# Two layers of a hybrid backbone on one core: latent products dealt by unit, one modulation block moved into the differential attention, three weight loads in another order

## The reference, cut to what matters

```
for l in range(2):
    mod = split(silu(c) @ ada_w[l] + ada_b[l], 6)        # c and c_ctx: shift, scale, gate, twice
    h = modulate(rmsnorm(x), mod[0], mod[1])             # 512 latent and 256 context tokens
    p = h @ w_in[l]                                      # SSD | differential attention | MLA columns
    d = for 4 heads, for each 128 queries:
        (softmax(q1 k1) - lam * softmax(q2 k2)) @ v      # latents see 768 keys, context sees 256
    cq, ckv, k_rope = latent columns of p                # 352 columns, and 16 of dt for the SSD
    a = softmax(q(cq) k(ckv, k_rope)) @ v(ckv)           # MLA, 4 heads
    s = bidirectional SSD over conv(p)
    x += mod[2] * rmsnorm([s, d, a] @ w_out[l])
    x += mod[5] * rmsnorm(expert_choice_ffn(modulate(rmsnorm(x), mod[3], mod[4])))
```

## Time and profile before

| | us |
|---|---|
| median of 3 runs | 2262.08 |
| lowest, highest | 2249.24, 2265.17 |
| the profiled execution's own time | 2259.05 |
| its span in the profile | 2257.2 |

### The profile page before, as it was taken

One profiled execution on the slowest core, in us unless ns is written; L12 is line 12 of the kernel. 1 busy time (PEld: TensorE's weight loads), 2 busy tenths in 40 slices (PEclk: granted clock), 3 DMA queues, 4 the chain that ended last, 5 costly groups with the idle time before them and its releaser, 6 DMA issues. The chain is left out here.

```text
span 2257.2 us, 25394 instructions
## 1 busy us (share of the span) xinstructions
PE 1962.4 (87%) x10710; PEld 947.2 (42%) x10710; DVE 618.3 (27%) x1149; ACT 522.1 (23%) x1039; POOL 211.1 (9%) x225
## 2 busy tenths in 40 slices
PE   4988999989959999999997999999794977777775
PEld 2655465544423333333334766655342322322222
DVE  2246462253241111111104355522623000000002
ACT  4134452434200000000005145523331000000002
POOL 1400000020011111111101000000100000000000
PEclk9988999989969999999998999999896998998988
DMA  9510401403069999999999113106117999999997
GB/s 345 154 37 1 168 1 41 184 1 110 31 231 380 402 394 394 399 396 394 395 389 321 38 38 135 34 1 224 38 57 297 368 401 401 401 406 401 401 401 261
DMA packets 166371, 534.54 MB, mean 237 GB/s; under 512 B 10600, under 2 KB 19122, under 8 KB 166258
## 3 DMA queue, kind: packets, MB, share of 16 engines
q1 hardware_dynamic: 148112, 487.39, 55.4%
q0 software_dynamic: 16480, 40.21, 6.4%
q10 hardware_dynamic: 1666, 5.31, 0.6%
HBM read 507.72 MB, written 25.17 MB: 236 GB/s over the span
## 5 line engine op out<-in xcount | busy, mean ns | idle before, releaser
L2504 PE MATMUL ps<-ring,arena 128*64 128x512 f32 x1056 | 252.1, 631 | 43.3 <-DMA ring<-in_w_up 29.0
L2504 PE MATMUL ps<-arena 128*64 128x512 f32 x892 | 217.0, 636 | 29.0 <-DMA arena<-in_w_up 29.0
L1914 PE MATMUL ps<-arena,ring 128*128 128x256 f32 (+1 forms) x640 | 208.6, 484 | 8.9 <-ACT arena L848 6.0
L2504 PEld LDWEIGHTS ps<-ring,arena 128*64 128x64 f32 x1056 | 81.3, 145 | 202.8 <-issue 202.8
L1914 PEld LDWEIGHTS ps<-arena,ring 128*128 128x128 f32 x640 | 121.6, 193 | 84.3 <-issue 66.0
L1835 DVE TENSOR_TENSOR arena<-arena,ps 128x512 f32<-128x512 f32 x32 | 22.0, 687 | 453.1 <-ACT arena L1208 453.1
L2433 PE MATMUL ps<-ring,arena 128*128 128x512 f32 x320 | 139.6, 594 | 0.8 <-DVE arena L1721 0.8
L2504 PEld LDWEIGHTS ps<-arena 128*64 128x64 f32 x892 | 70.3, 147 | 165.5 <-issue 165.5
L700 POOL DMA_INDIRECT expert_sums<-arena,small x32 | 52.4, 1639 | 855.7 <-ACT arena L1215 824.2
L2558 PE MATMUL ps<-ring,arena 128*64 128x512 f32 x544 | 122.3, 594 | 0.7 <-ACT arena L1222 0.7
L1208 ACT ACTIVATE arena<-ps 128x512 f32<-128x512 f32 x32 | 19.1, 597 | 439.5 <-PE ps L2504 439.5
(11 more groups left out here) (323 smaller groups left out, 2468.5 us busy)
## 6 DMA issues: line engine op xcount, KB each, us to landing
ring<-in_w_gate SPq DMA_DIRECT2D x35, 2048.0 KB, 21.4
ring<-in_w_down SPq DMA_DIRECT2D x34, 2048.0 KB, 22.5
ring<-in_w_up SPq DMA_DIRECT2D x31, 2048.0 KB, 15.4
arena<-in_w_down SPq DMA_DIRECT2D x25, 2048.0 KB, 23.2
ring<-in_ada_w SPq DMA_DIRECT2D x24, 2048.0 KB, 11.3
arena<-in_w_gate SPq DMA_DIRECT2D x24, 2048.0 KB, 20.6
arena<-in_w_up SPq DMA_DIRECT2D x23, 2048.0 KB, 14.9
ring<-in_w_in SPq DMA_DIRECT2D x6, 2048.0 KB, 13.9
```

What stands on the lines that cost most here:

```text
L1914: ins = mm(o[0:n, c0:c1], w[:, k, col:col + n], hT[:, k, c0:c1], start=k == 0, stop=k == KD - 1)
L2504: ins = mm(ps[0][hf * 64:hf * 64 + 64, col:col + 512], xl[e % 2][:, at:at + CAP_L], w[c][:, hf * 512:hf * 512 + 512], start=b + c == 0, st ...
```

## The change

Four things.

- `latent_products` no longer spreads each tile's eight products evenly. Each head (4 in layer 0, 4 in layer 1) does one tile, and a table deals its products to the head's units. In layer 0, where units 0 and 1 of a head are the context tiles: (0, 4, 3, 1, 0, 0), twice (2, 3, 2, 1, 0, 0), and (2, 2, 1, 1, 1, 1). Before it was (0, 1, 2, 1, 2, 2) and three times (1, 1, 2, 1, 1, 2). In layer 1: (0, 3, 3, 2) instead of (0, 2, 3, 3), the rest is (2, 2, 2, 2) as before.
- The DVE and ACT steps of the first pair of latents start in step 6 instead of step 1.
- Block 0 of part 1 moves from the stage between into the differential attention: its rows between the scores of unit 0 and the latent products of tiles 0 and 1, its columns behind those products. The job table and ACT's order follow; in ACT's order of the stage between, the rows of block 1 now come ahead of the wait for `o_ss`.
- Three loads change places: with block 0's buffer free early, SP issues the last block of part 1 during the differential attention, ahead of the X columns of w_in, and the B columns of w_in ahead of the third block of part 2.

```diff
-                        ("qk", 4), ("rot", 4), ("v", 2), ("datt", 4 * DH * q + 1),
-                        ("pre", 7), ("mq", 3), ("mrot", 2), ("mk", 2), ("mv", 2),
+                        ("qk", 4), ("rot", 4), ("v", 2), ("datt", 4 * DH * q + 2),
+                        ("pre", 6), ("mq", 3), ("mrot", 2), ("mk", 2), ("mv", 2),
...
-    order = [("score", 0, 0), ("score", 0, 1), ("latents", 0, 0), ("score", 1, 0), ("score", 1, 1)]
+    order = [("score", 0, 0), ("score", 0, 1), ("block", 0, 0), ("latents", 0, 0), ("score", 1, 0), ("score", 1, 1)]
...
-    ends = [(n - 1) * f // 4 + 1 for f in range(5)]
-    for f in range(4):
-        if ends[f] <= u < ends[f + 1]:
-            w, s = ends[f + 1] - ends[f], u - ends[f]
-            return 2 + f, 8 * s // w, 8 * (s + 1) // w
-    return None
+    h, i = divmod(u, n // DH)
+    share = {6: ((0, 4, 3, 1, 0, 0), (2, 3, 2, 1, 0, 0), (2, 3, 2, 1, 0, 0), (2, 2, 1, 1, 1, 1)),
+             4: ((0, 3, 3, 2), (2, 2, 2, 2), (2, 2, 2, 2), (2, 2, 2, 2))}[n // DH][h]
+    return (2 + h, sum(share[:i]), sum(share[:i + 1])) if share[i] else None
...
-    return [(1, (n - 1) // 2 + 2)[i] + k for k in range(4)] if i < 2 else [n] * 4
+    return [(6, (n - 1) // 2 + 2)[i] + k for k in range(4)] if i < 2 else [n] * 4
...
-    return (b, 7 + b, (12, 13, 15, 16)[b])[part]
+    return (b, (7, 8, 9, 11)[b], (12, 13, 14, 16)[b])[part]
...
-                for b, src in enumerate(srcs):
+                for b in [*range(10), 11, 10, 12, 13, 15, 14, *range(16, PRE_BLOCKS)]:
+                    src = srcs[b]
...
                 map_exps(0)
+                rows_out(l, 1, 0)
                 j = unit("latents", 0)
...
+                columns_out(l, 1, 0)
                 map_exps(1)
...
                 turned_latents(0)
+                rows_out(l, 1, 1)
+                turned_latents(1)
                 act.wait_ge(*a.next(S["o_ss"]))
                 rsqrt(rstd[:, 4 * q[0]:4 * NT], ssum[:, 4 * q[0]:4 * NT], DV, S["o_rstd"])
-                rows_out(l, 1, 0)
-                turned_latents(1)
-                columns_out(l, 1, 0)
-                rows_out(l, 1, 1)
+                columns_out(l, 1, 1)
+                rows_out(l, 1, 2)
                 turned_latents(2)
-                rows_out(l, 1, 2)
-                columns_out(l, 1, 1)
                 rows_out(l, 1, 3)
...
                 map_scores(0)
+                block_rows(l, 1, 0)
...
+                block_columns(l, 1, 0)
                 map_scores(1)
...
                 for k in (0, 4):
-                    block_rows(l, 1, 0, k)
+                    block_rows(l, 1, 1, k)
                     for n in range(k, k + 4):
                         turned_latent(1, n)
-                for k in (0, 4):
-                    block_rows(l, 1, 1, k)
-                    for c in (k // 2, k // 2 + 1):
-                        block_column(l, 1, 0, c)
-                for k in (0, 4):
-                    block_rows(l, 1, 2, k)
+                block_rows(l, 1, 2, 0)
+                block_columns(l, 1, 1)
+                block_rows(l, 1, 2, 4)
                 for n in range(8):
                     turned_latent(2, n)
-                block_rows(l, 1, 3, 0)
-                block_columns(l, 1, 1)
-                block_rows(l, 1, 3, 4)
+                block_rows(l, 1, 3)
```

More of the change, by code:

```diff
@@ L203, in ada_job @@
     if part == 1:
-        return JOBS[l, "pre"] + (1, 3, 4, 6)[b]
+        if b == 0:
+            return JOBS[l, "datt"] + diff_jobs(DH * len(query_tiles(l)))["block", 0, 0]
+        return JOBS[l, "pre"] + (1, 3, 5)[b - 1]
     if part == 2:
@@ L222, in latent_job @@
 def latent_job(l, i):
-    return JOBS[l, "pre"] + (0, 2, 5)[i]
+    return JOBS[l, "pre"] + (0, 2, 4)[i]
 def turn_job(t):
@@ L613, in block_used @@
                     j = tail_job(JOB[l, "tail"], n, "out", n - 1)
-                elif b in (11, 14):
-                    j = conv_job(l, 3 if b == 11 else 5)
+                elif b in (10, 15):
+                    j = conv_job(l, 3 if b == 10 else 5)
                 else:
@@ L625, in _ @@
                 srcs += [wi[:, :, c:c + n] for c, n in ((COL_QK, 512), (COL_V, 256), (COL_MLA, MLA_COLS))]
-                srcs += [aw[:, :, b * BLK:(b + 1) * BLK] for b in range(4, 8)]
+                srcs += [aw[:, :, b * BLK:(b + 1) * BLK] for b in range(4, 7)]
                 srcs += [wi[:, :, COL_X:COL_X + 512]]
-                srcs += [aw[:, :, b * BLK:(b + 1) * BLK] for b in range(8, 10)]
+                srcs += [aw[:, :, b * BLK:(b + 1) * BLK] for b in range(7, 11)]
                 srcs += [wi[:, :, COL_B:COL_B + 256]]
-                srcs += [aw[:, :, b * BLK:(b + 1) * BLK] for b in range(10, 12)]
+                srcs += [aw[:, :, 11 * BLK:12 * BLK]]
                 srcs += [wi[:, :, COL_Z:COL_Z + 512]]
                 srcs += [wo[:, :, b * BLK:(b + 1) * BLK] for b in range(2)]
-                for b, src in enumerate(srcs):
+                for b in [*range(10), 11, 10, 12, 13, 15, 14, *range(16, PRE_BLOCKS)]:
+                    src = srcs[b]
                     if l == 0 and b == 0:
@@ L2227, in _ @@
                 pair_values(np_ - 1)
-                w = arrived(wb + 11)
+                w = arrived(wb + 10)
                 feature_major(conv_job(l, 0), w, 0, P)
@@ L2235, in _ @@
                 feature_major(conv_job(l, 3), w, 3 * P, P)
-                w = arrived(wb + 14)
+                w = arrived(wb + 15)
                 feature_major(conv_job(l, 4), w, 0, P)
```

## The result

The changed kernel takes 2231.03 us (median of 9 runs, 2229.53 to 2237.74), the kernel before 2254.74 (9 runs, 2245.65 to 2267.20). The ratio is 0.9887, 95% interval 0.9861 to 0.9913: 1.1% faster, 25.5 us by the ratio and 23.7 by the medians, where 25.3 were forecast. The forecast time, 2236, counted from a median of 2262.08 over three runs of the kernel before; over nine runs it is 7 us lower. The profiled execution took 2232.26 us with a span of 2230.5, against 2259.05 and 2257.2, 26.7 less in span.

A forecast was written before the change was run, and what follows sets the result against it. PE was taken as the bound (busy 87% of the span), with DMA-bound experts unchanged. Terms of 15.5 - 2.1 + 9.0 + 2.9 = 25.3 us gave 2233.8 to 2236.8, stated as 2236; range 2222 to 2250.

The forecast's parts named there:

- Block 0: Moved early into the differential attention, its rows and columns cost 2.1 us in layer 0 and 2.4 in layer 1.
- stage between: Between differential and MLA attention: shorter PE waits for ACT's rows, 9.0 us less in layer 0, 6.4 in layer 1.
- context steps: Two steps per layer 0 head, bound by PE's own work: from 3.44 and 4.01 us to about 2.65 each.
- gated steps: Steps after latent scores, held to 4.35 us by ACT's exponentials; products moved there cost nothing in heads 2 and 3.
- rival 2: Layer 0's context steps don't shorten, held by DVE and ACT; 7.0 us not won, time 2244; chance 0.13.
- rival 1: The clock goes on falling once in every head; price 7.5 us, gain 17.8, time 2244; chance 0.20.
- rival 3: Half clock holds over the gated steps, some 50 us more over four heads, slower at 2284; chance 0.05.
- Loads: The three reordered loads: nothing gained, nothing lost.
- Layer 1: Stage between 6.4 us less, block 0 2.4 more, 0.6 and 0.5 lost in steps; 2.9 less in sum.
- slow second step: Layer 1's second step stays slow and gets one product more, at half clock: 0.6 us lost.
- The collision of the two pairs: In layer 1 DVE scales pair 0 and squares pair 1 in one step: 0.5 us lost.
- heads of layer 0: Differential attention: 17.9 us less if the clock holds, 15.5 with one fall of 2.4 left in the first head.

The follow-up runs named there:

- context_loaded: The changed kernel with heads 2 and 3 of layer 0 dealt (2, 2, 1, 0, 1, 2), three products back in context steps; 2246.96 us, 0.9942 to before.
- act_order: The kernel before, with ACT copying block 0's rows and the second pair of latents ahead of the norm's wait; 2250.89 us, 0.9983 to before.
- before_again: A copy of the kernel before, with no edit; 2255.48 us in one run.
- block_only: The changed kernel with the old dealing and old steps for the first pair of latents; 2240.96 us, 0.9949 to before.
- deal_only: The kernel before with only the new dealing and the later steps for the first pair of latents; 2244.74 us, 0.9945 to before.
- old_loads: The changed kernel with the three loads in their old order and old places in the ring; 2230.16 us, 0.9884 to before.
- deal_act_order: The kernel before with the new dealing, later first-pair steps and ACT's earlier copies; block 0 and loads stay as before; 2235.04 us, 0.9904 to before.
- first_filled: The changed kernel with only the first head of layer 0 dealt (2, 3, 2, 1, 0, 0); 2229.01 us, 0.9864 to before.
- last_emptied: The changed kernel with only the last head of layer 0 dealt (2, 3, 2, 1, 0, 0); 2231.49 us, 0.9886 to before.
- fuller: The changed kernel with all four heads of layer 0 dealt (2, 3, 2, 1, 0, 0); 2229.93 us, 0.9879 to before.
- empty_second: The changed kernel with heads 2 and 3 of layer 0 dealt (3, 0, 2, 3, 0, 0), leaving the second step empty; 2238.87 us, 0.9917 to before.
- fuller_again: A copy of the kernel with all four heads of layer 0 dealt (2, 3, 2, 1, 0, 0), no edit; 2231.24 us in one run.

## Why the prediction was right

**The gate and the context steps.** The mechanism was right. 4.35 us for gated steps was measured as 4.34 to 4.45, context steps as 2.76 where 2.65 was forecast; heads 2 and 3 took 23.0 instead of 22.7, 0.3 less won in each. context_loaded shows the price of a product in a context step (1.95 us for three, with the clock held), so rival 2 is out. What the dealing gives without any help of the clock follows from heads that kept it: 24.96 us with the old dealing (the third of act_order), 23.06 with the new, so 1.9 of the 4.2 us that each of these heads got shorter in the two profiles; the other 2.3 were falls of that one execution.

**The clock.** The direction was right, the certainty wrong. The prediction took 2.4 us a head as a fixed part of the old dealing. It differs from execution to execution: with the old dealing heads 2 to 4 show 20.4 us of half clock in the first profile, 6.8 in before_again and act_order, 3.4 in block_only. With the new dealing these heads show none in eight profiles (changed, deal_only, old_loads, deal_act_order, first_filled, last_emptied and both of fuller), while empty_second and context_loaded, which have longer waits in heads 2 and 3, have 10.2 each. So rival 1 and rival 3 fell.

How long the waits must be is less plain than the contrast suggests. Over the 14 profiles the waits of 2.48 to 2.67 us came with a fall during or just behind them in 5 of 5 places (three in stages between, two in empty_second), the 1.78 us of the old dealing in 8 of 12, and the first head's wait of 1.96 or 1.61 in 11 of 11, against none of 3 where it is 0.37. The waits of 1.16 and 1.34 us that the new dealing has in the last head were followed by none in 7 profiles, but nearly the same waits were followed by one in one head of context_loaded and not in the next. The one fall left in the first head cost 7.67 - 4.35 = 3.3 us and not 2.4; it covers the step with four products.

**Block 0 and the stage between.** Right in size: 2.17 us paid where 2.1 was forecast (2.65 for 2.4 in layer 1), 8.7 won where 9.0 was, in layer 1 6.05 for 6.4. act_order shows what won it: 5.7 of the 8.7 came with ACT's order, the wait of 2.67 us and the half clock behind it. The block's own move gives the other 3.0 in the stage and takes 2.17 of them back.

**Loads.** Right: they are worth nothing, as old_loads shows.

**Layer 1.** The term that was mis-sized. 2.9 us less was forecast; from the first scores to the up projections it is 103.18 to 97.14, 6.0 less, and 1.7 more in the MLA attention. The forecast kept the slow second step and charged 0.6 more for it; in the changed kernel the step took 5.07 instead of 7.72, and the half clock in layer 1's MLA attention wasn't there. The collision of the two pairs cost 0.46 in one step (4.90), as forecast. The step's clock went with the block's early place in 13 of 14 profiles, which the prediction did not think of.

**The sum.** It is in part luck that it came out so near. In the two profiles the heads of layer 0 won 14.0 us instead of 15.5, the stage 0.3 less than forecast, the layer 1 terms 7.7 instead of 2.9, and 1.5 us were lost in places that the forecast left alone: 26.7 instead of 25.3. These errors have opposite signs. The pair of profiles is luck as well, since the kernel before happened to have 20.4 us of half clock in heads 2 to 4 in the one that the forecast was made from.

The Trainium skill, "TensorE: Matmul & The Clock Gate", section "A second HAM failure mode: psum-queue depth-cycling", has a kernel in which PE idles briefly and often between groups of products and its clock goes back and forth for that. The heads of the old dealing agree with it, with falls behind waits of 1.78 us; the new dealing, which keeps a short wait in nearly every gated step, has none in heads 2 to 4. The same page's section "HAM oscillation" names long gaps as the cause; no wait here is that long, and the clock fell all the same.

## What to carry to other kernels

Deal movable work by each step's slack, and work the slack out as the step's gate (here the loop from scores through maxima and exponentials back to the slots) less the engine's own work: a product in a gated step cost nothing, the same product in a step bound by PE cost all of its 0.6 to 0.8 us. Look at the order of the engine that is waited for before moving work of the one that waits: of the 8.7 us of the stage between, 5.7 came with two lines of ACT's order. Where the clock falls behind waits of one or two microseconds in some executions and not in others, one profile misleads: look at several, and compare a stretch that no edit touches to see how much two profiles differ by themselves.

## What the runs showed of the hardware that was not expected

The same wait (1.78 us ahead of the same scores) was followed by 6.8 us at 1.2 GHz in one execution and by none in another. The spread of the runs doesn't show this by itself. The kernel before lies between 2243.1 and 2272.9 over all its runs here, the changed one between 2229.5 and 2237.7 and old_loads between 2229.5 and 2231.8, but deal_only (2234.4 to 2247.2), first_filled (2223.4 to 2235.2) and last_emptied (2229.5 to 2244.7) have the new dealing and spread over 12 to 15 us.

And the clock fell, in both executions of fuller, in a stretch in which PE had been busy for 16.83 of 16.84 us (10.07 of 10.08 in the stage between and 6.76 of 6.76 behind it; 16.86 of 16.87 in fuller_again) and stayed busy. last_emptied ran the same instructions with the same spacing at 2.4 GHz. A wait of PE is not the only thing that comes ahead of a fall. What does in that place is open.
